# Attention scores of two layers as three one-pass products of 64-row tiles, with q and k split into high and low parts

## The reference, cut to what matters

```python
def stick_breaking_attention(q, k, v):
        z = jnp.einsum('bqhd,bkhd->bhqk', q_blk, k, preferred_element_type=jnp.float32) * scale
        log_keep = jnp.where(earlier, jax.nn.log_sigmoid(-z), 0.0)
        log_after = lax.cumsum(log_keep, axis=3, reverse=True) - log_keep
        weight = jnp.where(earlier, jnp.exp(jax.nn.log_sigmoid(z) + log_after), 0.0)
def differential_attention(q1, q2, k1, k2, v, lam):
        def attn_map(qb, kk):
            s = jnp.einsum('bqhd,bkhd->bhqk', qb, kk, preferred_element_type=jnp.float32) * scale
            return jax.nn.softmax(jnp.where(visible, s, NEG_INF), axis=-1)
        a = attn_map(q1_blk, k1) - lam * attn_map(q2_blk, k2)
```

## Time and profile before

| what | value |
|---|---|
| time of three runs | 2187.49, 2189.53, 2189.46 us; median 2189.46 |
| span of the profiled execution, first to last instruction | 2186.7 us |
| its own time | not listed apart from the three; the median lies 2.8 us above the span |
| PE busy in the span | 2133.8 us, 98%, 14982 matmuls |
| DVE, ACT, POOL busy | 57%, 47%, 10% |
| layer 0's attention | about 917 to 1164 us from the span's start |
| layer 1's attention | about 1591 to 1802 us |

### The profile page before, as it was taken

How to read it: one execution, slowest core, us unless ns; L and a number is a source line. 1 busy time by engine, 2 the same in 40 slices (tenths; PEclk the granted TensorE clock), 3 DMA queues, 4 the chain that set the end, 5 groups by cost and what they waited for, 6 DMA issues and landing times.

```text
span 2186.7 us, 35850 instructions
## 1 busy us (share of the span) xinstructions
PE 2133.8 (98%) x14982; PEld 1685.9 (77%) x14982; DVE 1247.0 (57%) x2247; ACT 1038.3 (47%) x2012; POOL 224.2 (10%) x240
## 2 busy tenths in 40 slices
PE   8999999999999999999999999999999999999999
PEld 6777676777777887877777888888777777888887
DVE  6667677666654456655557542445577676443442
ACT  6656565566555235656655332233455544332331
POOL 0112221221220010100001000000101001000000
PEclk9999999999999999999999999999999999999999
DMA  4221211221214432211112222222211112222222
GB/s 177 99 79 63 78 65 50 89 68 50 97 50 153 142 135 78 70 67 59 58 39 82 97 97 97 97 97 97 82 62 63 63 59 97 97 97 96 97 97 77
DMA packets 36226, 186.68 MB, mean 85 GB/s; under 512 B 4560, under 2 KB 4944, under 8 KB 16992
## 3 DMA queue, kind: packets, MB, share of 16 engines
q1 hardware_dynamic: 36064, 184.38, 24.7%
HBM read 172.80 MB, written 7.90 MB: 83 GB/s over the span
## 4 chain that ended last, share of the span: by engine, by line
PE 89%; DVE 6%; ACT 3%; issue 2%; DMA 0%; SPq 0%; POOL 0%; DVEq 0%; ACTq 0%
PE ps L1834 88%; PE ps L1837 1%; ACT arena L2779 1%; DVE spl L2286 1%; ACT spl L2782 0%; ACT hh L2779 0%; DVE x L2644 0%; DMA raw<-wstream 0%; DVE x L2402 0%; DVE arena L2587 0%; DVE x L2573 0%; DVE arena L2485 0%; DVE arena L2569 0%; DVE hl L2595 0%; ACT on_t L2779 0%
## 5 line engine op out<-in xcount | busy, mean ns | idle before, releaser
L1834 PE MATMUL ps<-hh,spl 128*128 128x512 f32 (+1 forms) x3152 | 1024.1, 399 | 6.4 <-DVE hl L2577 2.1
L1834 PEld LDWEIGHTS ps<-hh,spl 128*128 128x128 f32 x3152 | 584.6, 189 | 139.5 <-issue 19.6
L1834 PE MATMUL ps<-hl,spl 128*128 128x512 f32 (+1 forms) x1568 | 620.8, 396 | 0.0
L2286 DVE TENSOR_TENSOR spl<-raw,spl 128x512 fp32r<-128x512 f32 x596 | 421.2, 731 | 153.6 <-ACT spl L2782 152.4
L1834 PE MATMUL ps<-arena_r,spl 128*128 128x512 f32 x1968 | 467.2, 392 | 10.3 <-DVE arena_r L2298 8.4
L1834 PEld LDWEIGHTS ps<-arena_r,spl 128*128 128x128 f32 x1968 | 371.1, 189 | 89.6 <-issue 10.5
L2782 ACT ACTIVATE spl<-raw 128x512 fp32r<-128x512 f32 x596 | 345.3, 619 | 143.9 <-PE ps L1834 138.8
L1834 PEld LDWEIGHTS ps<-hl,spl 128*128 128x128 f32 x1568 | 295.9, 189 | 63.0 <-issue 9.1
L1834 PE MATMUL ps<-arena 32*32 32x32 f32 (+6 forms) x5664 | 218.2, 224 | 16.8 <-issue 10.5
L2779 ACT ACTIVATE arena<-arena 128x512 f32<-128x512 f32 (+3 forms) x220 | 142.3, 648 | 189.7 <-DVE arena L2649 140.8
L1834 PEld LDWEIGHTS ps<-arena 32*32 32x32 f32 (+4 forms) x5664 | 126.2, 116 | 98.2 <-issue 79.4
(11 more groups left out here) (258 smaller groups left out, 2117.0 us busy)
## 6 DMA issues: line engine op xcount, KB each, us to landing
raw<-wstream SPq DMA_DIRECT2D x148, 1024.0 KB, 4.9
arena<-spill SPq DMA_DIRECT2D x17, 256.0 KB, 5.3
GS<-g_rows SPq DMA_DIRECT2D x16, 256.0 KB, 3.4
spill<-x SPq DMA_DIRECT2D x14, 256.0 KB, 2.0
arena<-arena SPq DMA_DIRECT2D x18, 128.0 KB, 2.2
x<-xT SPq DMA_DIRECT2D x4, 512.0 KB, 6.4
spill<-arena SPq DMA_DIRECT2D x8, 256.0 KB, 2.0
x<-xT SPq DMA_DIRECT2D x1, 2048.0 KB, 7.8
```

The costliest lines, as they stand in the source:

```text
L1834: return pe.matmul(out, lhsT, rhs, start=start, stop=stop, skip_group_check=True)
L2286: tt(spl[:, p % 2, 1, c], raw[:, p % 2, c], spl[:, p % 2, 0, c].bitcast(F32), ALU.subtract) \
```

## The change

q and k of both layers are split, after they are made, into a high part (ACT, step `qs_hi`, a copy to fp32r) and a low part (DVE, step `qs_lo`, the difference, in place), and each score product becomes three fp32r products of the same 64-row tiles. The new steps come from a new lane, which the planner runs with the priority of `prep`, and the scores wait for both low parts. The arena grows from 41 to 48 tiles for the extra parts, and room is made for it by a smaller scratch area for dynamic transfers. Five semaphores of an early step are merged into one counter (not shown). The planner's guess for a score step falls from 0.86 to 0.65 us at 512 columns.

```diff
+    def halves_lane(layer, which, m, made, iqk):
+
+        o.behind(made)
+        yield "AC"
+        o.add("qs_hi", layer, which, m, cost=[("AC", AC_B)]).iqk = iqk
+        yield "DV"
+        o.add("qs_lo", layer, which, m, cost=[("DV", DV_B)]).iqk = iqk
+
     def stick_front(m):
-        while m not in qk_of:
+        while m not in qk_of or ("qs_lo", 0, "q", m) not in o.at or ("qs_lo", 0, "k", m) not in o.at:
             yield
-            st = o.add("st_z", m, kb, cost=[("PE", 0.3 + 0.86 * f)], u=u)
+            st = o.add("st_z", m, kb, cost=[("PE", 0.3 + 0.65 * f)], u=u)
...
+            o.spawn("kspl", halves_lane(0, "k", m, st, iqk))
...
+        o.spawn(which + "spl", halves_lane(1, which, m, st, iqk))
     def score_lane(m):
-        while ("br_out", "q", m) not in o.at or ("br_out", "k", m) not in o.at:
+        while ("qs_lo", 1, "q", m) not in o.at or ("qs_lo", 1, "k", m) not in o.at:
...
-        NA = 41
+        NA = 48
...
-                    q_, k_ = qk_of[q.iqk]
-                    for b in range(2):
-                        r = slice(64 * b, 64 * b + 64)
-                        mm(psum[u.b + b][:, 0:n], k_[r, kb * 128:kb * 128 + 128], q_[r, kb * 128:S], True, False)
+                        w.wait_ge(sem("qs_lo"), max(at["qs_lo", 0, c, m].n for c in "qk"))
+                    qh, ql, kh, kl = (part(0, c, q.iqk) for c in "qk" for part in (qk_hi, qk_lo))
+                    for j, (k_, q_) in enumerate(((kh, qh), (kh, ql), (kl, qh))):
+                        for b in range(2):
+                            r = slice(64 * b, 64 * b + 64)
+                            mm(psum[u.b + b][:, 0:n], k_[r, kb * 128:kb * 128 + 128], q_[r, kb * 128:S], j == 0, False)
...
+                elif kind == "qs_lo":
+                    layer, which, m = q.key
+                    lo = qk_full(layer, which, q.iqk)
+                    w.wait_ge(sem("qs_hi"), at[("qs_hi",) + q.key].n)
+                    tt(qk_lo(layer, which, q.iqk), lo, qk_hi(layer, which, q.iqk).bitcast(F32), ALU.subtract) \
...
+                    copy(qk_hi(layer, which, q.iqk), qk_full(layer, which, q.iqk)).then_inc(sem("qs_hi"), 1)
```

More of the change, by code:

```diff
@@ L1235, in arrange @@
     qk_of = {}
+    def halves_lane(layer, which, m, made, iqk):
[4 more added lines that the diff above has]
+        o.add("qs_lo", layer, which, m, cost=[("DV", DV_B)]).iqk = iqk
     def stick_front(m):
-        while m not in qk_of:
+        while m not in qk_of or ("qs_lo", 0, "q", m) not in o.at or ("qs_lo", 0, "k", m) not in o.at:
             yield
-        o.behind(o.at["st_q", m], o.at["st_k", m])
+        o.behind(o.at["qs_lo", 0, "q", m], o.at["qs_lo", 0, "k", m])
         for kb in range(4):
@@ L1443, in score_lane @@
             o.now = 0.0
-            o.behind(o.at["br_out", "q", m], o.at["br_out", "k", m], p_old)
+            o.behind(o.at["qs_lo", 1, "q", m], o.at["qs_lo", 1, "k", m], p_old)
             yield "PE"
-            st = banked("df_s", m, qb, cost=[("PE", 0.25 + 0.86 * f), ("DV", 0.15 + 1.08 * f), ("AC", 0.25 + 0.42 * f),
+            st = banked("df_s", m, qb, cost=[("PE", 0.25 + 0.65 * f), ("DV", 0.15 + 1.08 * f), ("AC", 0.25 + 0.42 * f),
                                              ("AC", 0.25 + 0.42 * f)], bank=sbp)
@@ L1649, in build, with qk_hi, qk_full, qk_lo @@
         v8, o8 = wide(0, 8), [A(8 + i) for i in range(8)]
-        qk_of = [(A(16), A(17)), (A(18), A(19)), (A(38), A(39))]
+        qk_at = [[(16, 17, 18, 19), (38, 39, 41, 42), (43, 44, 45, 46)], [(16, 17, 18, 19), (23, 24, 41, 42), (43, 44, 45, 46)]]
+        def qk_hi(layer, which, i):
+            return R(qk_at[layer][i][2 * (which == "k")])
+        def qk_full(layer, which, i):
+            return A(qk_at[layer][i][2 * (which == "k") + 1])
+        def qk_lo(layer, which, i):
+            return R(qk_at[layer][i][2 * (which == "k") + 1])
         sp_of, wt_of = ([A(i, 2) for i in ids] for ids in ((20, 22, 24), (26, 28)))
@@ L2223, in tensor @@
                     if qb == 0:
[L2224 to L2228, removed]
+                        w.wait_ge(sem("qs_lo"), max(at["qs_lo", 1, c, m].n for c in "qk"))
+                    qh, ql, kh, kl = (part(1, c, q.iqk) for c in "qk" for part in (qk_hi, qk_lo))
+                    for i, (q_, k_) in enumerate(((qh, kh), (qh, kl), (ql, kh))):
+                        for j in range(2):
+                            r = slice(64 * j, 64 * j + 64)
+                            mm(psum[u.b + j][:, 0:n], q_[r, qb * 128:n], k_[r, 0:n], i == 0, False)
                     for j in range(2):
@@ L2607, in vector @@
                         w.wait_ge(sem("rstd"), at["rstd", "attn0"].n)
[L2608 removed]
+                    stt(out=qk_full(0, "q", q.iqk), in0=psum[q.u.b][:, :], scalar=0.125, in1=SQ["attn0"][2], op0=ALU.mult,
                         op1=ALU.mult).then_inc(drained[q.u.b], 1)
@@ L2740, in vector @@
                         full(q.old.u)
-                    tt(qk2_of[q.iqk][q.which == "k"], t_, rs, ALU.mult).then_inc(sem("br_out"), 1)
+                    tt(qk_full(1, q.which, q.iqk), t_, rs, ALU.mult).then_inc(sem("br_out"), 1)
                 elif kind == "df_s":
@@ L2898, in scalar @@
                     full(u)
-                    f(g3(beta), db, ACT.Exp, scale=-1.0).then_inc(sem("gate_eb"), 1)
+                    f(g3(beta), db, ACT.Exp, scale=-1.0).then_inc(sem("gate_act"), 1)
                     empty(u)
@@ L3111, in scalar @@
                       scale=rs_col[:, q.tb:q.tb + 1]).then_inc(drained[q.u.b], 1)
+                elif kind == "qs_hi":
+                    layer, which, m = q.key
+                    if layer == 0:
+                        empty(at["st_" + which, m].u)
+                    else:
+                        w.wait_ge(sem("br_out"), at["br_out", which, m].n)
+                    copy(qk_hi(layer, which, q.iqk), qk_full(layer, which, q.iqk)).then_inc(sem("qs_hi"), 1)
                 elif kind == "st_e":
```

31 lines of the change are left out of this document (14 added, 17 removed).

## The result

The change makes the kernel slower by a little: 2193.99 us in the median of 8 runs against 2188.05 of the kernel before, a ratio of 1.0028 (95% interval 1.0018 to 1.0039), 5.9 us. The profiled execution spans 2192.0 us, 5.3 more than that of before. PE is busy for less time than before (2132.2 us instead of 2133.8), so it waits for more than the products save.

The account below looks back on a forecast made before the run. PE bounds the kernel, so only matmuls saved and waits added count: -4.3 + 2.5 + 2.0 + 7.7 + 1.8 = +9.7 us on 2189.5, giving 2199 us; own range 2194 to 2205, 8 in 10 within 2191 to 2210.

Parts of the forecast that it names:

- the same: Rival: three queue waits vanish, layer 1's end waits 7.1 us, clock stays up; +2.8 us, 2192; chance 0.17.
- st_w(4,2): Layer 0: PE waits about 1.6 us for low parts that DVE makes only after taking out k(5)'s projection.
- st_z(2,2): Layer 0: PE waits 0.9 us for a bank, a 2.3 us chain against 1.4 us of matmuls.
- os_lo(3): Layer 1, ahead of the output projection: PE waits behind eight DVE operations; +2.0 us, bounds 0 and 3.
- The score products: Score pairs of both layers: three fp32r products behave like the float32 pair, same 0.21 us fixed; -4.3 us in all.
- The rival in which weight loads show: Score pairs: second and third products each add a load of about 0.11 us; 2209 us; chance 0.12.
- The faster rival: Score pairs: the fixed 0.21 us, and about 0.1 on entering, go with float32; 2180 us; chance 0.05.
- Layer 0: Layer 0's attention: PE waits at two places in the new order; +2.5 us, bounds 0 and 3.5.
- The end of layer 1: Behind layer 1's last score pair: 47 moved `mul` no longer cover the chain; PE waits +7.7 us, bounds 7.1 and 9.2.
- The clock: End of layer 1: idleness brings one more episode of lower granted clock; +1.8 us, bounds 0 and 5.4.

Follow-up runs that it names:

- one_product: The change with only the high-by-high product of each score made, the two products with a low part left out; 2176.26 us in a single run.
- order_only: The change's order of steps with float32 scores and no splitting instructions; 2196.45 us, ratio 1.0037 to the kernel before.
- tail_order: The change with all its instructions, layer 1 alone reordered (lead up to 3 us, scores' lane ahead); 2183.36 us, ratio 0.9978 to the kernel before.
- order_44b: The change with all its instructions, four head pairs first, planner's settings changed in both layers (layer 1 up to 4 us); 2179.29 us, 0.9968 of the kernel before.
- layer0_only: The change in layer 0 alone, layer 1 with float32 scores and no splitting; 2187.95 us, ratio 1.0002 to the kernel before.

## Why the prediction was right, and where it was off

Forecast were 2199 us, 9.7 above the kernel before, and slower with a chance of 0.77. It became slower, by 5.9, inside the range of 2191 to 2210 and at the lower edge of the forecast's own 2194 to 2205. Of the 5.2 us between forecast and result, 1.4 are the base: the forecast built on a median of 2189.46 of three runs, and eight gave 2188.05. The change itself, 5.9, lies about midway between the forecast's 9.7 and the 2.8 of the rival "the same", so the time alone does not tell these two apart. The traces do: the three waits that the rival lets vanish, at `st_w(4,2)`, at `st_z(2,2)` and for `os_lo(3)`, are all there.

- **The score products.** -4.3 forecast, -4.9 measured; 0.89, 0.735, 0.57 and 0.48 for a pair became 0.90, 0.72, 0.55 and 0.48 in the median. That fp32r pairs behave like float32 pairs, with the same fixed part, was right. The rival in which weight loads show falls twice, by the pairs and by `one_product`. The strict rule of the Trainium skill ("TensorE: Matmul & The Clock Gate", "The mechanism"), that a load overlaps only matmuls of another row group, does not hold for these pairs: each further product has weights of its own for the same rows and adds 0.23 or 0.11 us, the plain pitch. The paragraph ahead of it, which also allows a load into a background weight buffer, agrees with that. The faster rival falls too: the 0.20 stays without float32.
- **Layer 0.** +2.5 forecast for two places. At `st_w(4,2)` 1.6 became 1.45, by the chain that was named:

```profile
1061.31 0.69 DVE L2634 TENSOR_TENSOR arena<-ps,arena 128x512 f32<-128x512 f32 x1
1061.92 0.41 DVE L2653 TENSOR_TENSOR arena_r<-arena,rv_r 128x256 fp32r<-128x256 f32 x1
1062.25 0.42 DVE L2653 TENSOR_TENSOR arena_r<-arena,st_r 128x256 fp32r<-128x256 f32 x1
...
1062.72 0.38 PE L1857 MATMUL ps<-rv_r,const_r 128*128 128x256 f32 x1 [1.45 <-DVE arena_r L2653]
```

  At `st_z(2,2)` 0.9 became 0.75. Two places were missed: 0.55 at `st_w(3,1)`, where a wide `st_p` and an `os_lo` stand right ahead of `st_l` on DVE, and 0.18 at another `st_w`, where a wide `st_p` does. Together it is 2.9 instead of 2.5.
- **Layer 1, `os_lo(3)`.** 2.0 forecast, 1.31 measured. The price of the five operations was right, 2.05 us from the maximum's start to that of `qs_lo`, where 2.0 were forecast. What the forecast left out stands on PE: behind the nine `mul` come two `df_t`, which wait 0.15 us and take 0.41, and PE does them while DVE's chain runs:

```profile
1757.28 0.96 DVE L2773 TENSOR_REDUCE small<-ps 128x2 f32<-128x768 f32 x1 [3.06 <-PE ps L1857]
1759.33 0.69 DVE L2639 TENSOR_TENSOR arena_r<-arena,arena_r 128x512 fp32r<-128x512 f32 x1
1759.56 0.41 PE L1860 MATMUL ps<-cst,arena 128*128 128x128 f32 x2 [0.15 <-DVE arena L2788]
1761.28 0.74 PE L1857 MATMUL ps<-arena_r,spl 128*128 128x512 f32 x2 [1.31 <-DVE arena_r L2545]
```

- **The end of layer 1.** 7.7 forecast, 7.16 measured, in three pieces. From the pair to pair 7's first `mul` it took 17.8 us, where 16.2 were forecast and 19.3 had been; PE's own part of that is 10.65 instead of 8.5, with the clock down for part of it. `df_o` alone, at 3.40 instead of 2.32, is 1.1 of the 1.6 us that the chain took longer than forecast. With the 10.7 us of 47 `mul` that are no longer in it the stretch loses 17.81 - (19.33 - 10.7 - 0.16) = 9.3, against 7.7 + 1.8 (waits and clock) of the sum. `order_only` and `tail_order` show the mechanism from both sides.
- **The clock.** One drop more in layer 1 was forecast, and the trace has three instead of two. That the count fits is in part luck: at the end of the layer the clock fell twice,

```profile
1795.20:1799.20 4.00, 3.97 (x10) 2.25 (x11) 0.00 (x0) 1.11 (x2) 0.00 (x0) 0.58 0.00 0
1806.50:1809.50 3.00, 2.92 (x7) 2.34 (x8) 1.19 (x3) 0.44 (x1) 0.00 (x0) 0.51 0.00 0
```

  while the drop that before had behind the wait of 1.50 us at 1580.95 (0.50 from 1582 to 1584 us) went with that wait (1.00 there now). It also differs from run to run: the eight runs of the change go from 2191.2 us at a mean clock of 0.997 to 2197.8 at 0.994.
- **The step that failed** is the sum itself: it added the new waits and took the old ones over unchanged. The list of waits was read for layer 0 alone. In layer 1 the kernel before had five, 0.87 + 1.50 + 0.83 + 0.74 + 1.24 = 5.2 us; in the new order 1.2 us of such waits stand in the layer. That is 4.0 us, most of the 4.4 by which the forecast lay above the trace. The prediction had the thought only in its rival "the same", where the moved `mul` fill small waits. The 47 `mul` that left the end cannot themselves have done it: all five waits end by 1762.60, and the first `mul` of the output projection starts at 1766.65 before and at 1757.08 now. At the first of the five, 50 `mul` of the projections of q and k now stand ahead of the waiting step instead of 47, and 0.87 became 0.20, which is the 0.68 us of three `mul`. For the other four it was not followed what came to stand ahead of them.

The account of layer 1 is then -2.5 for the pairs, +1.3 and +7.2 for the new waits, -4.0 for the old, and 1.4 to 1.7 (an estimate) for the further drop of the clock, in sum +3.4 to +3.7; measured is +4.87. The remaining 1.2 to 1.5 us are spread over ordinary matmuls and not explained, nor are 0.5 in layer 0.

## What to carry to other kernels

When a change makes a planner order everything anew, price the order apart from the change: list the waits of the whole stage before, ask of each whether the new list still has it, and count what stands beside the last chain of each stage (here 61, 14 and 64 `mul` beside some 17 to 21 us of chain). To learn which of the two it is, run the new order without the new work and the new work in another order; both are short edits. And before a change gets the credit for a gain, give the kernel before the same search: here that alone was worth 8 us, and the change's best order 9.

## What the runs showed of the hardware that was not expected

Of the traces in which PE had just waited 1.82 or 1.83 us at the start of layer 1, the clock fell in some and not in others. Here are the wait and the stretch behind it, first in the kernel before, then in `order_44b` (columns as in the earlier trace rows):

```profile
1554.80:1556.70 1.90, 0.07 (x2) 0.04 (x1) 1.81 (x5) 0.72 (x2) 0.00 (x0) 1.00 0.00 0
1556.70:1562.00 5.30, 5.30 (x15) 3.87 (x16) 2.06 (x4) 1.75 (x3) 1.79 (x1) 0.68 0.42 125
```

```profile
1550.00:1551.90 1.90, 0.07 (x2) 0.03 (x1) 1.81 (x5) 0.71 (x2) 0.00 (x0) 1.00 0.00 0
1551.90:1556.50 4.60, 4.60 (x19) 3.47 (x20) 2.10 (x5) 1.76 (x3) 1.09 (x1) 1.00 0.37 77
```

It is the same wait, and the mean clock behind it is 0.68 in the one and 1.00 in the other. In the first it was partly at the lower of its two levels (1.2 instead of 2.4 GHz), and 0.32 of 5.30 us is 1.7 us of PE's work. In `layer0_only` and `tail_order` even 2.2 us at this place left the clock at 1.00, and in the change the same 2.2 did not (0.59 from 1557 to 1561 us). So the price of a wait of about 2 us is the wait, and sometimes 1.7 us on top.
